# Late attention of a two-block transformer on one Trainium2 core: attention units of two heads instead of one, with the query norms made in three groups

## The reference, cut to what matters

```python
q_all = u @ b_w_q                                   # 12 dilated heads and 4 memory heads of 64
q = rms_norm(q, q_gain)                             # over the 64 features of each head
# dilated heads: 3 groups of 4 heads, dilation 1, 4 and 16, keys and values shared from the layer before
logits = where(mask, q . k / sqrt(64) + bias, NEG_INF)
m = max(logits); p = exp(logits - m); l = sum(p); o = p @ v / l; lse = m + log(l)
y_dil = sum over groups of softmax(lse over groups) * o
# memory heads: 256 memory rows, the same for all tokens
y_mem = softmax(rms_norm(q) . k / sqrt(64)) @ v
x = x + concatenate(y_dil, y_mem) @ b_w_out
```

## Time and profile before

| what | value |
|---|---|
| median of 3 runs | 3764.86 us (3764.27 to 3769.51) |
| the profiled execution | 3761.94 us, of which 3760.1 us are the span from its first to its last instruction |
| PE, DVE, ACT, POOL busy | 95%, 48%, 33%, 12% of the span |
| share of the chain that ended last | PE 83%, DVE 9% |
| mean granted TensorE clock | 0.972 of full speed |

### The profile page before, as it was taken

One profiled execution on the slowest core, in us unless ns is written; L12 is line 12 of the kernel. 1 busy time (PEld: TensorE's weight loads), 2 busy tenths in 40 slices (PEclk: granted clock), 3 DMA queues, 4 the chain that ended last, 5 costly groups with the idle time before them and its releaser, 6 DMA issues.

```text
span 3760.1 us, 41635 instructions
## 1 busy us (share of the span) xinstructions
PE 3562.6 (95%) x16796; PEld 2779.4 (74%) x16796; DVE 1823.5 (48%) x2553; ACT 1256.4 (33%) x1978; POOL 467.0 (12%) x338
## 2 busy tenths in 40 slices
PE   3999999799999899999899989999999999889999
PEld 2765777575677788887788877788877886668887
DVE  6944345643436744347654564433555336334433
ACT  2333342433333422234233333222343224333221
POOL 1000001000001311012332302101101001001100
PEclk9999999999999999999999999999999999669999
DMA  4531122221112232232100003332222222003222
GB/s 188 188 113 51 51 84 79 73 84 51 53 49 85 96 107 92 94 112 97 51 1 1 1 23 103 102 95 91 94 84 89 92 88 78 7 23 101 94 93 89
DMA packets 83470, 295.91 MB, mean 79 GB/s; under 512 B 9424, under 2 KB 12624, under 8 KB 81232
## 3 DMA queue, kind: packets, MB, share of 16 engines
q1 hardware_dynamic: 82704, 289.05, 23.7%
q10 hardware_dynamic: 576, 4.19, 0.3%
HBM read 284.56 MB, written 8.65 MB: 78 GB/s over the span
## 4 chain that ended last, share of the span: by engine, by line
PE 83%; DVE 9%; issue 2%; ACT 2%; POOL 1%; DMA 0%; ACTq 0%; DVEq 0%; SPq 0%; POOLq 0%
PE acc L473 61%; PE aux L1510 5%; PE acc L1427 2%; PE acc L2196 2%; PE acc L1533 2%; PE acc L2208 1%; PE aux L2178 1%; DVE w_lo L384 1%; PE acc L2212 1%; PE aux L1412 1%; PE aux L1521 1%; DVE square_sums L2619 1%; DVE square_sums L2498 1%; DVE late_norm L2619 1%; PE aux L1787 0%
## 5 line engine op out<-in xcount | busy, mean ns | idle before, releaser
L473 PE MATMUL acc<-op_hi,w_hi 128*128 128x512 f32 x2624 | 1106.3, 422 | 50.7 <-DVE op_lo L1078 22.7
L473 PE MATMUL acc<-op_hi,w_lo 128*128 128x512 f32 x2624 | 1041.4, 397 | 0.0
L473 PE MATMUL acc<-op_lo,w_hi 128*128 128x512 f32 x2624 | 1039.9, 396 | 0.0
L377 ACT ACTIVATE w_hi<-raw 128x1024 fp32r<-128x1024 f32 (+2 forms) x476 | 494.0, 1038 | 1495.2 <-PE acc L473 1494.1
L384 DVE TENSOR_TENSOR w_lo<-raw,w_hi 128x1024 fp32r<-128x1024 f32 (+2 forms) x476 | 576.6, 1211 | 234.9 <-ACT w_hi L377 234.5
L473 PEld LDWEIGHTS acc<-op_hi,w_hi 128*128 128x128 f32 x2624 | 497.7, 190 | 208.7 <-issue 71.7
L473 PEld LDWEIGHTS acc<-op_hi,w_lo 128*128 128x128 f32 x2624 | 497.0, 189 | 117.4
L473 PEld LDWEIGHTS acc<-op_lo,w_hi 128*128 128x128 f32 x2624 | 499.0, 190 | 110.1 <-issue 13.0
L473 PE MATMUL acc<-ffn_hi,w_hi 128*128 128x512 f32 x800 | 316.1, 395 | 0.0
L473 PE MATMUL acc<-ffn_lo,w_hi 128*128 128x512 f32 x800 | 315.7, 395 | 0.0
L473 PE MATMUL acc<-ffn_hi,w_lo 128*128 128x512 f32 x800 | 315.7, 395 | 0.0
(11 more groups left out here) (476 smaller groups left out, 4531.6 us busy)
## 6 DMA issues: line engine op xcount, KB each, us to landing
raw<-in_w SPq DMA_DIRECT2D x436, 512.0 KB, 3.4
late_ada<-in_ada SPq DMA_DIRECT2D x32, 512.0 KB, 4.4
raw<-in_w SPq DMA_DIRECT2D x32, 384.0 KB, 3.0
x<-in_x SPq DMA_DIRECT2D x2, 2048.0 KB, 10.2
ada<-in_ada SPq DMA_DIRECT2D x4, 1024.0 KB, 22.8
ada<-in_ada ACTq DMA_DIRECT2D x4, 1024.0 KB, 16.4
x_mid<-x SPq DMA_DIRECT2D x16, 256.0 KB, 3.0
x<-x_mid SPq DMA_DIRECT2D x2, 2048.0 KB, 8.4
```

What stands on the lines that cost most here:

```text
L377: act.activation(self.w_hi[g % 2][:, 0:k, :], self.raw[s][:, 0:k, :], ACT.Copy).then_inc(self.split_hi.handle, 1)
L473: mm = pe.matmul(self.bank(s, g), w[:, k, :], a[:, k, 0:s.n], start=(k == 0 and q == 0), stop=(k == k_tiles - 1 and q == 2))
```

## The change

Nothing in the computed result changes. Four things do:

- `GroupNorms` replaces `HeadNorms` for the queries. The tiles go in groups of two, three and three. For each tile a matmul with a window of constants adds the means of its two heads as two rows to one bank of four or six rows. One root and one reciprocal then serve the group, and two matmuls of 64 output columns a tile spread the factors back to 128 partitions.
- `PairAttention` replaces `Attention`. A unit is both heads of a tile and 128 tokens: 8 memory units and 24 dilated ones (18 with 128 keys, 6 with 256). Both heads' query-key products come first, from partitions 0 to 63 and 64 to 127 into two different banks, and then both biases. The values of both heads go to one bank and are kept with one DVE instruction.
- The queue's order is new. Dilated units have two pairs of score banks, one turn bank, one bank for values, and DVE copies the turned probabilities. Memory units have one pair of score banks. Memory units are spaced 3.0 us in the plan, dilated ones 1.5 or 2.5 us. `DilatedPairs` asks for all memory results before its first scores.
- The plan's k step is 0.8 us instead of 0.9, its pause is 68 us instead of 98, and the banks and places of small tiles are dealt anew.

The diff, cut to its core (empty added lines are left out too):

```diff
              "blk": row // HD == col // HD,
+             "window": np.stack([(i < HD) * (c == 4) + (i >= HD) * (c == 5) for c in range(10)], 1) / HD,
...
+class GroupNorms(Stage):
...
+        def roots():
+            for j, g, i, src, n in self.tiles():
+                if i < n - 1:
+                    continue
+                yield self.at[j] + 2.6
+                act.wait_ge(*self.summed.ge(j + 1))
+                if g:
+                    act.wait_ge(*self.spreaded.ge(j + 1 - n))
+                act.activation(self.factor[0:2 * n, :], self.sums[0:2 * n, :], ACT.Sqrt, bias=self.eps[0:2 * n, :]
+                               ).then_inc(*self.rooted.inc())
...
+        def sums():
+            for j, g, i, src, n in self.tiles():
+                yield self.at[j] + 1.5
+                if g and i == 0:
+                    pe.wait_ge(*self.rooted.ge(g))
+                pe.wait_ge(*self.squared.ge(j + 1))
+                pe.matmul(self.sums[0:2 * n, :], core.c("window")[:, 4 - 2 * i:4 - 2 * i + 2 * n], self.square[j % 2],
+                          start=(i == 0), stop=(i == n - 1), skip_group_check=True).then_inc(*self.summed.inc())
...
+        def spreads():
+            for j, g, i, src, n in self.tiles():
+                yield self.at[j - i + n - 1] + 8.4 + 2.0 * i
+                if i == 0:
+                    pe.wait_ge(*self.inverted.ge(g + 1))
+                if j:
+                    pe.wait_ge(*self.made.ge(j))
+                for e in range(2):
+                    mm = pe.matmul(self.spread[e * HD:(e + 1) * HD, :],
+                                   column(core.c("ident")[0:2 * n, 2 * i + e:2 * i + e + 1], HD),
+                                   self.factor[0:2 * n, :], start=True, stop=True)
+                mm.then_inc(*self.spreaded.inc())
...
+        def work():
+            for j, g, i, src, n in self.tiles():
+                if i == 0:
+                    yield self.at[j + n - 1] + 4.2
+                    dve.wait_ge(*self.rooted.ge(g + 1))
+                    dve.reciprocal(self.factor[0:2 * n, :], self.factor[0:2 * n, :]).then_inc(*self.inverted.inc())
+                yield self.at[j - i + n - 1] + 9.4 + 2.0 * i
+                dve.wait_ge(*self.spreaded.ge(j + 1))
+                self.finish(dve, j, self.spread[:, :]).then_inc(*self.made.inc())
...
+class PairAttention(Stage):
...
+        def scores():
+            ring = len(self.score_banks)
+            for u, unit in enumerate(units):
+                yield self.at[u]
+                for count in self.ready if u == 0 else ():
+                    pe.wait_ge(*count)
+                for count in unit["ready"]:
+                    if not u or count not in units[u - 1]["ready"]:
+                        pe.wait_ge(*count)
+                if u >= ring:
+                    pe.wait_ge(*self.exped.ge(2 * (u - ring + 1)))
+                n, bias = unit["keys"], unit.get("bias")
+                for e in range(2):
+                    lhsT, rhs = unit["scores"][e]
+                    mm = pe.matmul(self.scores_bank(u, e)[:, 0:n], lhsT, rhs, start=True, stop=not bias,
+                                   skip_group_check=True)
+                    if not bias:
+                        mm.then_inc(*self.scored.inc())
+                for e in range(2) if bias else ():
+                    pe.matmul(self.scores_bank(u, e)[:, 0:n], core.c("ident"), bias[e], start=False, stop=True,
+                              skip_group_check=True).then_inc(*self.scored.inc())
+        def turns():
+            m = len(self.turn_banks)
...
+                yield self.turn_at(u)
+                for count in self.turn_ready if u == 0 else ():
+                    pe.wait_ge(*count)
+                if u >= m:
+                    pe.wait_ge(*self.copied.ge(u - m + 1))
+                for e in range(2):
+                    pe.wait_ge(*self.exped.ge(2 * u + e + 1))
+                    for b in range(0, n, P):
+                        mm = pe.transpose(self.turn_banks[u % m][:, e * n + b:e * n + b + P],
+                                          probs[:, u % 2, e * n + b:e * n + b + P], core.c("ident"))
+                mm.then_inc(*self.turned.inc())
...
+                yield self.value_at(u)
+                for count in self.out_ready if u == 0 else ():
+                    pe.wait_ge(*count)
+                pe.wait_ge(*self.copied.ge(u + 1))
+                if u >= m:
+                    pe.wait_ge(*self.kept.ge(u - m + 1))
+                for e in range(2):
+                    for b in range(0, n, P):
+                        mm = pe.matmul(self.out_banks[u % m][:, e * HD:(e + 1) * HD],
+                                       self.probs_t[:, u % 2, e * n + b:e * n + b + P], unit["values"][e][b // P],
+                                       start=(b == 0), stop=(b == n - P), skip_group_check=True)
+                mm.then_inc(*self.summed.inc())
...
+                    yield self.exp_at(u, e)
+                    if e == 0 and u >= 2:
+                        act.wait_ge(*self.turned.ge(u - 1))
+                        if "stats" not in unit:
+                            act.wait_ge(*self.kept.ge(u - 1))
+                    act.wait_ge(*self.maxed.ge(2 * u + e + 1))
+                    act.activation(self.probs[:, u % 2, e * n:(e + 1) * n], self.scores_bank(u, e)[:, 0:n], ACT.Exp,
+                                   bias=self.stat(u, 0, e), accum_out=self.stat(u, 1, e)).then_inc(*self.exped.inc())
...
+class MemPairs(PairAttention):
...
+        self.at = [start + pace * u for u in range(len(self.units))]
+        self.end = self.at[-1] + 7.0
...
+class DilatedPairs(PairAttention):
...
+        self.at = [start]
+        for unit in self.units:
+            self.at.append(self.at[-1] + (1.5 if unit["keys"] == P else 2.5))
+        self.at += [self.at[-1] + 1.5, self.at[-1] + 3.0]
+        self.end = self.value_at(len(self.units) - 1) + 1.2
...
+    def max_at(self, u, e):
+        return self.at[u] + 0.6 + 0.3 * e
+    def exp_at(self, u, e):
+        return self.at[u] + 1.15 + 0.55 * e
+    def turn_at(self, u):
+        return self.at[u + 1] + 1.0
+    def copy_at(self, u):
+        return self.at[u + 1] + 1.45
+    def value_at(self, u):
+        return self.at[u + 2] + 0.95
+    def keep_at(self, u):
+        return self.at[u + 2] + 1.7
...
+        groups = [[q[:, tiles[j], :] for j in js] for js in ((0, 1), (2, 3, 4), (5, 6, 7))]
...
+        self.memory = MemPairs(core, "late_mem", units, ([aux[0:2]], aux[2:3], aux[3:4]), probs, probs_t, small, "act")
...
+        self.dilated = DilatedPairs(core, "late_dil", units, ((aux[0:2], aux[2:4]), acc[1:2], acc[2:3]), probs, probs_t,
+                                    None, "dve")
...
-        units = self.attention.units
-        mem, end = 4 * MEM_HEADS, taken[-1]
-        t0 = taken[1] + 11.0
-        pace = max(1.9, (end - t0) / 20)
-        self.attention.at = [t0 + pace * u for u in range(mem)]
-        now = self.attention.at[-1] + pace
-        for u in range(mem, len(units)):
-            tile = self.Q_ORDER[2 + (u - mem) // 8]
-            now = max(now, taken[self.Q_ORDER.index(tile)] + 11.0)
-            self.attention.at.append(now)
-            now += 2.0 if units[u]["keys"] > P else 1.4
-        self.mem_at = max(self.attention.t(mem, 9.0), end + 2.0)
-        self.mix_at = [self.attention.t(mem + 24, 6.0), now + 9.0]
-        self.end = self.mix_at[1] + 14.0
+        self.memory.times(taken[1] + 14.0, 3.0)
+        self.memory.ready = []
+        self.dilated.times(max(taken[4] + 17.0, taken[-1] + 2.0, self.memory.end + 1.0))
+        self.dilated.ready = [self.memory.kept.ge(len(self.memory.units))]
+        self.dilated.turn_ready = [linear.last_freed(at)]
+        self.dilated.out_ready = [self.norm_q.rooted.ge(3)]
+        self.memory.turn_ready = self.memory.out_ready = []
+        per = 4 * DIL
+        self.mem_at = max(self.memory.end + 0.5, taken[-1] + 2.5)
+        self.mix_at = [self.dilated.at[per * (j + 1) - 1] + 2.6 for j in range(2)]
+        self.end = self.dilated.end + 12.0
...
+    def small(self, j):
+        return self.core.acc[0 if j else 3]
 
     def bank(self, i):
-        return self.core.acc[i % 2]
+        return self.core.acc[0 if i < 2 else 3]
...
-                            ready=lambda k: to_queries.ready()(k), late=NORM_LATE, banks=core.acc[0:2], step=0.9))
+                            ready=lambda k: to_queries.ready()(k), late=NORM_LATE, banks=core.acc[0:2], step=0.8))
     segments.append(Segment(KD, late.pair, Residual(lambda j: 1.0, to_last), ready=late.ready,
-                            banks=[*core.acc[2:4], *core.acc[0:2]], pause=98.0))
+                            banks=[*core.acc[2:4], *core.acc[0:2]], pause=68.0))
```

More of the change, by code:

```diff
@@ L2824, in __init__ @@
                 tile = 2 * g + j
-                for e in range(2):
-                    head = DIL_HEADS * g + 2 * j + e
-                    rows = slice(e * HD, (e + 1) * HD)
```

(42 more changed lines are left out.)

179 lines of the change are left out of this document (148 added, 31 removed).

## The result

The changed kernel takes 3710.03 us (median, 3705.24 to 3713.19) against 3764.57 for the kernel before on the same chip: a ratio of 0.9854, 95% interval 0.9837 to 0.9871. The saving is 54.5 us; the forecast was 70 (3695, range 3681 to 3727). The profiled execution took 3713.19 us, span 3711.4.

The account below looks back on a forecast made before the run. A loop of scores, values, keep and exp, mostly at the lower clock, was taken to bound the kernel. Query stage -8 and the rest -61.7 gave -70: 3692 from the profiled execution, forecast 3695 us as median, range 3681 to 3727.

Parts of the forecast that it names:

- The price of a strided pair: Dilated stage: a strided 128-key pair takes 2.0 us at the full clock, 3.1 us at the lower one.
- The second head's products for nothing: In the pairs: the second head's query-key product overlaps the first's on other array rows and is counted as free.
- The start stall: After the last query matmul: dilated units wait on memory results, root, reciprocal, low part and transposes; 10.5 us, bounds 3 to 10.5.
- The tail: From the last values to the output projection's first matmul: 9.8 us before, less 0.8, so 9.0 us.
- The sum over the region: Query stage through the output projection's first matmul: 8 us and 61.7 us saved, 70 us together.
- the clock, 3.5 us: After the start stall: the clock falls, and the first 256-key pairs cost up to twice until it returns; +3.5 us.
- the rest: From the last query matmul to the output projection's first matmul: 83.6 us against 145.3 before.
- The rival with a low clock in part: Dilated pairs: clock stays low for eight strided pairs and some long ones only; 3704 to 3712 us, chance 0.13.
- the query stage: Making query tiles: fewer reciprocals on DVE remove idle time, 87.2 to 79 us, 8 us gained; bounds nothing or 11.
- kept full: Dilated pairs: a PE with back-to-back work may keep the full clock; its price is within the pairs' 50.5 us.
- the lack of overlap: Rival: the two heads' products do not overlap; 9.7 us in the pairs, 4.4 in memory scores, 3709 us, chance 0.12.

Follow-up runs that it names:

- run 10: The changed kernel once more, unchanged, for a second profile: 3709.02 us, ratio 0.9844.
- run 1: The kernel before with only the change's new 10-column constant added to its table of constants, read by nothing: 3772.43 us, ratio 1.0014.
- Run 4: The changed kernel with the query norms one tile at a time as before, instead of grouped: 3701.68 us, ratio 0.9824.
- run 3: The changed kernel with a dilated pair's products in the order head 0, its bias, head 1, its bias: 3762.32 us, ratio 0.9979.
- run 5: The kernel before, its dilated units' exp no longer waiting for the keep of the unit four earlier: 3750.67 us, ratio 0.9957.
- run 6: The changed kernel with each head's product followed by its bias, plus eight unused matmuls ahead of the first dilated scores: 3765.15 us, ratio 0.9996.
- Run 7: The changed kernel with three unused 128 x 512 matmuls filling the start stall: 3702.74 us, ratio 0.9825.

## Why the prediction was right, and where 15 us went

The measured 3710 lies within the range, but above the 3684 to 3703 that the forecast held likeliest. One term came out 3 us better than forecast, and one was missing and one mis-sized the other way; that they partly cancel is luck.

**Right.** The price of a strided pair, 2.0 and 3.1 us forecast, 2.02 and 3.09 measured. The second head's products for nothing: 0.76 us for four passes. The start stall, 10.5 against 9.8, with the reciprocal, `late_lo` and the transposes in the order named. The tail, 9.0 against 8.9. The sum over the region: 70 against 67.2 in the first profile, made of 11.0 in the query stage where 8 were forecast and 56.2 behind it where 61.7 were.

**Mis-sized: the clock, 3.5 us.** "Until it is back the first 256-key pairs cost up to twice": it was not back with them. The low stretches in the pairs lasted 17 and 34 us in two profiles of one kernel. At 3.09 against 2.02 us a strided pair, a stretch at the lower clock loses 35% of its length, more with 256-key pairs: 6 us and more in the first profile, and the second is 6.9 us longer than that. So the rest took 89.1 and 96.0 us where 83.6 were forecast, 5.5 and 12.4 more. The first mix's two waits, 0.66 and 0.86 us, were not in the sum either. The rival with a low clock in part (0.13; 3704 to 3712, eight strided pairs and some long ones) describes run 10, and its time is the measured one: it came truer than the forecast (0.61).

**Missing: what a longer table of constants does.** No term stood for it; run 1 measures 5.3 us. Region and table together, for the two profiles of the changed kernel: (67.2 + 60.3) / 2 - 5.3 = 58, against 54.5 and, in run 10, 58.7 (1.56% of 3764.57) measured.

**Wrong in its cause: the query stage.** I let the grouped norms take the stage's idle time, 8 us in all. The stage went from 88.0 to 77.0, the 11 that I had set as its bound. Run 4 shows that the pairs do that without the grouped norms, to 74.7: these save 5.3 us of idle time and cost 7.7 of PE's.

**Wrong in an argument.** I expected the clock from a PE "kept full". Runs 3, 5 and 6 have it full at 0.50. It was in the view by stages already, though only with waits beside it. What after has and these lack is both heads' products in the array at once. That the overlap itself is what holds the clock is argued, not shown, and it is not enough: after was busy for 23.90 of 23.90 us at 0.64, run 10 for 30.80 of 30.80 at 0.50. A rival that no run tests is the share of the time that strided products take, 0.76 of 2.02 us in a pair of after and 1.5 of 2.97 with the heads in turn; it was at 0.50 among the unstrided first pairs of runs 3 and 6 too, which speaks against that as the only cause.

**Wrong in a bound: the lack of overlap.** 9.7 us, from 0.42 for a head's two strided passes. The earlier trace rows showed 0.75 for them. The price of the order alone is 0.95 us a strided pair at the full clock, and with the clock that goes with it 52 us (run 3 against after), the largest single effect of this study.

The Trainium skill, "TensorEngine Tiling (Array Packing)", Key Properties, says that different tiles of the array can load and multiply in parallel. The traces agree: 0.76 us for the four passes of two heads, 0.75 for the two of one. The Trainium skill, "TensorE: Matmul & The Clock Gate", section "A second HAM failure mode: psum-queue depth-cycling", ties a swinging clock to small idles between groups of matmuls. Run 7 fits it, with 6 to 11 us for a filled stall. Runs 5 and 6, at 0.50 with PE busy for 57.39 of 58.00 and 91.24 of 92.10 us, show a low clock almost without idles, of which that section does not tell.

## What to carry to other kernels

Two products on half the array's rows each, issued next to each other into different banks, cost one; with the 128-row bias product between them the overlap was gone and, here, most of the full clock with it. Read the clock beside the busy share: a PE busy all the time may still run at 0.50, and then taking out waits helps (16 us in run 5) without bringing the clock back. An idle gap just ahead of such a stretch may be worth filling. Before taking a cost off an engine, ask which wait it still causes once the rest of the change stands: with the pairs in place, taking the reciprocals away cost more than it gave (run 4).

## What the runs showed of the hardware

A strided product (tokens 16 bytes apart, 64 rows, two passes of 128 columns) takes 0.75 to 0.77 us at either clock (3325.65 to 3326.40 at 1.00, 3318.51 to 3319.28 at 0.50 in run 6), for one head or for two at once; four passes over adjacent tokens take 0.43 at the full clock (3269.97 to 3270.40 in after). Its length did not follow the clock.

The same GpSimd product takes a mean of 1136 ns, or 1310 with its mask 40 bytes further on (1134 to 1138 in the six profiles with the masks in their old place, 1309 to 1315 in the eight others); nothing in its shape changed.

DVE's reciprocal of 6 x 512 takes 3.33 us, that of 128 x 512 3.34: fewer partitions saved nothing.

One kernel, same instructions, had 17 us at the lower clock in the pairs in one profile and 34 in another, and its query stage began 11 us apart, with about 113 and 85 us at the lower clock ahead of it. One profile of each kernel is not enough to place a difference of 10 us.
